# Cross attention beside a projection: earlier fetches, exponentials ahead of the last split, the next projection's operands split inside its last step

## The reference, cut to what matters

```python
s = einsum('bhsd,bhmd->bhsm', heads(xq), heads(mk)) * 128 ** -0.5
p = softmax(s, axis=-1)
xo = einsum('bhsm,bhmd->bhsd', p, heads(mv))
xo = merge_heads(rms_norm(xo, xattn_norm_w))
mixed = concatenate([gla_o, hgrn_o, xo], axis=-1)
mixed = mixed * silu(gate)
x = x + einsum('bse,ed->bsd', mixed, w_out)
```

## Time and profile before

| | us |
|---|---|
| median of 3 runs (2594.1 to 2599.44) | 2598.51 |
| the profiled execution's own time | 2591.98 |
| its span | 2590.2 |
| PE busy | 2432.3 (94%) |
| DVE, ACT, POOL busy | 1178.3, 910.4, 757.6 |
| idle time of PE before L1450, L1440 and L403 at this place | 14.6, 8.7, 6.8 |

### The profile page before, as it was taken

How to read it: one execution, slowest core, us unless ns; L and a number is a source line. 1 busy time by engine, 2 the same in 40 slices (tenths; PEclk the granted TensorE clock), 3 DMA queues, 4 the chain that set the end, 5 groups by cost and what they waited for, 6 DMA issues and landing times.

```text
span 2590.2 us, 42170 instructions
## 1 busy us (share of the span) xinstructions
PE 2432.3 (94%) x16392; PEld 2131.3 (82%) x16392; DVE 1178.3 (45%) x2536; ACT 910.4 (35%) x1685; POOL 757.6 (29%) x725
## 2 busy tenths in 40 slices
PE   6999989999997898899999999999999999798986
PEld 5778968798786898899998898777898777586786
DVE  3001359999994332400000155346435434666535
ACT  4214554444443332311212233433334333444321
POOL 3112325455641121312223133243223322221123
PEclk9999999999998999999999999999999999899998
DMA  4334334333335123232222313313321323636511
GB/s 181 123 110 153 114 134 147 129 127 124 114 131 211 58 81 114 82 113 93 92 95 97 126 50 122 110 62 109 119 92 71 127 92 125 219 138 221 205 50 65
DMA packets 153707, 306.01 MB, mean 118 GB/s; under 512 B 11456, under 2 KB 75584, under 8 KB 142288
## 3 DMA queue, kind: packets, MB, share of 16 engines
q1 hardware_dynamic: 89296, 215.77, 23.8%
q10 hardware_dynamic: 64256, 88.10, 9.5%
HBM read 204.22 MB, written 99.61 MB: 117 GB/s over the span
## 4 chain that ended last, share of the span: by engine, by line
PE 66%; issue 17%; DVE 9%; DMA 3%; POOL 3%; ACT 2%; ACTq 0%; SPq 0%; POOLq 0%; DVEq 0%
PE bank L392 10%; PE bank L394 9%; PE bank L393 9%; PE bank L403 7%; PE bank L404 7%; PE bank L405 7%; PE bank L1974 3%; PE bank L1954 2%; POOL w_lo L358 2%; PE bank L1374 1%; PE bank L1943 1%; PE bank L666 1%; DVE w_lo L358 1%; DVE rec_z L1109 1%; DMA rec_pre<-mixT 1%
## 5 line engine op out<-in xcount | busy, mean ns | idle before, releaser
L403 PE MATMUL bank<-w_hi,at_hi 128*128 128x256 f32 x2432 | 703.9, 289 | 15.0 <-DVE at_lo L2154 7.0
L404 PE MATMUL bank<-w_lo,at_hi 128*128 128x256 f32 x2432 | 691.2, 284 | 0.0
L405 PE MATMUL bank<-w_hi,at_lo 128*128 128x256 f32 x2432 | 691.1, 284 | 0.0
L392 PE MATMUL bank<-at_hi,w_hi 128*128 128x512 f32 x1472 | 609.4, 414 | 22.5 <-DVE at_lo L1574 8.5
L394 PE MATMUL bank<-at_hi,w_lo 128*128 128x512 f32 x1472 | 579.5, 394 | 0.0
L393 PE MATMUL bank<-at_lo,w_hi 128*128 128x512 f32 x1472 | 578.2, 393 | 0.0
L358 POOL TENSOR_TENSOR w_lo<-w_raw,w_hi 128x2048 fp32r<-128x2048 f32 x69 | 318.1, 4610 | 863.7 <-ACT w_hi L371 863.7
L403 PEld LDWEIGHTS bank<-w_hi,at_hi 128*128 128x128 f32 x2432 | 470.6, 194 | 29.2 <-issue 19.9
L404 PEld LDWEIGHTS bank<-w_lo,at_hi 128*128 128x128 f32 x2432 | 470.1, 193 | 0.6
L405 PEld LDWEIGHTS bank<-w_hi,at_lo 128*128 128x128 f32 x2432 | 469.6, 193 | 0.0
L423 ACT ACTIVATE stage<-bank 128x512 f32<-128x512 f32 x272 | 162.4, 597 | 640.7 <-PE bank L394 337.1
(11 more groups left out here) (251 smaller groups left out, 2969.2 us busy)
## 6 DMA issues: line engine op xcount, KB each, us to landing
w_raw<-in_weights SPq DMA_DIRECT2D x84, 1024.0 KB, 6.6
feat<-stage ACTq DMA_DIRECT2D x152, 256.0 KB, 2.0
tok<-stage ACTq DMA_DIRECT2D x104, 256.0 KB, 2.2
stage<-feat SPq DMA_DIRECT2D x32, 256.0 KB, 3.2
x<-in_x SPq DMA_DIRECT2D x4, 1024.0 KB, 9.7
w_mem<-in_w_mem SPq DMA_DIRECT2D x4, 1024.0 KB, 11.6
logg<-gate_g ACTq DMA_DIRECT2D x8, 512.0 KB, 2.8
rec_b<-logg SPq DMA_DIRECT2D x16, 256.0 KB, 4.7
```

Of the source, the lines that this page charges most:

```text
L392: nc.tensor.matmul(ps_gemm[i % 2], wh, ah, start=(k == 0), stop=False)
L403: nc.tensor.matmul(o, ah, wh, start=(k == 0), stop=False)
L404: nc.tensor.matmul(o, ah, wl, start=False, stop=False)
L405: last = nc.tensor.matmul(o, al, wh, start=False, stop=(k == KT - 1))
```

## The change

It touches five places:

- In the recurrence's last head SP issues load 3, keys, values and loads 4 to 6, each behind a wait of its own (`gate_silu`, `r_o`, `fill_lo`), ahead of the last store to `mixT`. ACT and DVE split load 3 together with loads 0 to 2.
- After the barrier SP issues the first head's queries, then the first half of X, then waits for the last store and issues the first head's gates, load 7, queries and gates of the second head, and the weights. ACT and DVE split loads 4 to 6 ahead of the first step; load 7 and the recurrence's last weight split move behind the first step's exponentials.
- The projection's parts per step are 2, 3, 1, 2 in the first and 1, 3, 1, 3 in the others.
- The next projection's first token half is split inside the last step (`rest_high`, `rest_low`), three row groups ahead of the sums of squares on ACT and ahead of the normed rows on DVE, five behind them. The rows of the last two heads are read from `ca_mx` itself and no longer go through DRAM. The second token half follows in phase 4.
- The loops of phase 3 are written out instead of turning on a register.

```diff
-        beside_cross = Beside(0, HEADS // 2, gemm_out[0], [1, 3, 1, 3] * 4)
+        beside_cross = Beside(0, HEADS // 2, gemm_out[0], [2, 3, 1, 2] + [1, 3, 1, 3] * 3)
...
                 fill_load(sp, mix_slots, mixT[0:D, :], FILLED0, range(3))
+                sp.wait_ge(gate_silu, 2 * (2 * HEADS))
+                fill_load(sp, mix_slots, mixT[0:D, :], FILLED0, range(3, 4))
+                sp.wait_ge(r_o, head * 8 + (6 + 8))
+                sp.dma_start(cmk[:].rearrange("p h m -> p (h m)"), mk_dram).then_inc(c_mem, 16)
+                sp.dma_start(cmv[:].rearrange("p t n -> p (t n)"), mv_dram).then_inc(c_mem, 16)
+                fill_load(sp, mix_slots, mixT[0:D, :], FILLED0, range(4, 7))
...
-                    fill_low(dve, mix_slots, FILLED0, range(3))
+                    fill_low(dve, mix_slots, FILLED0, range(4))
...
-                    fill_high(act, mix_slots, 0, range(3))
+                    fill_high(act, mix_slots, 0, range(4))
...
         def p3_sp(sp):
-            fill_load(sp, mix_slots, mixT[0:D, :], FILLED0, range(3, 4))
-            sp.dma_start(cmk[:].rearrange("p h m -> p (h m)"), mk_dram).then_inc(c_mem, 16)
+            block_stored(sp, REC_BLOCKS - 4)
+            queries_in(sp, 0, 0)
+            sp.dma_start(X[:, :, 0:HALF], I["x"].rearrange("(t p) d -> p t d", p=P)[:, :, 0:HALF]).then_inc(x_in, 16)
             sp.wait_ge(r_st, 16 * (2 * 2 * HEADS + 1))
             block_stored(sp, REC_BLOCKS - 2)
-            cross_load(sp, 0, 0)
-            sp.dma_start(cmv[:].rearrange("p t n -> p (t n)"), mv_dram).then_inc(c_mem, 16)
-            sp.dma_start(X[:, :, 0:HALF], I["x"].rearrange("(t p) d -> p t d", p=P)[:, :, 0:HALF]).then_inc(x_in, 16)
-            cross_load(sp, 0, 1)
+            gates_in(sp, 0, 0)
+            fill_load(sp, mix_slots, mixT[0:D, :], FILLED0, range(7, LOADS))
+            queries_in(sp, 0, 1)
+            gates_in(sp, 0, 1)
             beside_cross.weights(sp, 0)
-            fill_load(sp, mix_slots, mixT[0:D, :], FILLED0, range(4, LOADS))
...
+            sp.wait_ge(fill_lo, FILLED1)
+            fill_load(sp, rest_slots, mixT[D:2 * D, :], FILLED1, range(2))
+            for j in range(2):
+                sp.wait_ge(c_st[j], 16 * 2)
+            fill_load(sp, rest_slots, mixT[D:2 * D, :], FILLED1, range(2, 3))
             beside_cross.weights(sp, 1)
...
         def p3_act(act):
-            fill_high(act, mix_slots, 0, range(3, 4))
             all_products(act, gemm_rec)
-            split_high(act, *rec_block(REC_BLOCKS - 1))
-            fill_high(act, mix_slots, 0, range(4, LOADS))
-            with act.Fori(0, PAIRS) as it:
+            fill_high(act, mix_slots, 0, range(4, 7))
+            for it in range(PAIRS):
...
+                    if first:
+                        fill_high(act, mix_slots, 0, range(7, LOADS))
+                        split_high(act, *rec_block(REC_BLOCKS - 1))
                     beside_cross.results(act, it, 4 * n + 1)
...
+                    if final:
+                        rest_high(act, 0, range(3))
...
+                    if final:
+                        rest_high(act, 0, range(3, KT))
                     beside_cross.results(act, it, 4 * n + 3)
...
         def p3_dve(dve):
-            fill_low(dve, mix_slots, FILLED0, range(3, 4))
-            low_after(dve, REC_BLOCKS * 4 - 1)
-            fill_low(dve, mix_slots, FILLED0, range(4, LOADS))
-            with dve.Fori(0, PAIRS) as it:
+            fill_low(dve, mix_slots, FILLED0, range(4, 7))
+            for it in range(PAIRS):
...
+                    if first:
+                        fill_low(dve, mix_slots, FILLED0, range(7, LOADS))
+                        low_after(dve, REC_BLOCKS * 4 - 1)
                     beside_cross.sums(dve, it, 4 * n + 1)
...
+                    if final:
+                        rest_low(dve, 0, range(3))
                     dve.wait_ge(c_rs, it * 8 + (2 * n + 2))
...
+                    if final:
+                        rest_low(dve, 0, range(3, KT))
                     beside_cross.sums(dve, it, 4 * n + 3)
...
+        def rest_slice(k, h):
+
+            return cmx[:, k - 6, half(h)] if k >= 6 else rest_slots[k // 2][:, k % 2, :]
+
+        def rest_high(act, h, ks):
+
+            for k in ks:
+                if k == 0:
+                    act.wait_ge(tile_done, 4 * (gemm_out[0][0].first + gemm_out[0][0].n) + 6 + 2 * h)
+                if k < 6:
+                    act.wait_ge(part_in[k // 2], 16 * (h + 4))
+                else:
+                    act.wait_ge(c_mx, 4 * (PAIRS - 1) + (4 + 2 * (k - 6) + h + 1))
+                nc.scalar.activation(at_hi[:, k, half(h)], rest_slice(k, h), ACT.Copy).then_inc(fill_hi, 1)
...
         def p4_act(act):
-            all_products(act, gemm_out[0])
-            fill_high(act, rest_slots, 1, range(LOADS))
+            rest_high(act, 1, range(KT))
...
         def p4_dve(dve):
-            all_products(dve, gemm_out[0])
-            fill_low(dve, rest_slots, FILLED1, range(LOADS))
+            rest_low(dve, 1, range(KT))
```

More of the change, by code:

```diff
@@ L1424, in cross_load, with gates_in @@
             sp.dma_start(cq[:, j, :], feat1[XQ + head * P:XQ + (head + 1) * P, :]).then_inc(c_in[j], 16)
+        def gates_in(sp, it, j):
+            head = it * 2 + j
             sp.dma_start(cg[:, j, :], feat1[C_AT + head * P:C_AT + (head + 1) * P, :]).then_inc(c_in[j], 16)
         def p3_pe(pe):
-            with pe.Fori(0, PAIRS) as it:
+            ready = lambda k, h: FILLED0 + h * KT + k
+            for it in range(PAIRS):
                 for j, hf, n in halves():
-                    head = pe.snap(it * 2 + j)
-                    col = pe.snap(it * (2 * P) + j * P)
-                    beside_cross.products(pe, it, 4 * n, lambda k, h: FILLED0 + h * KT + k)
-                    if n == 0:
+                    head = it * 2 + j
+                    beside_cross.products(pe, it, 4 * n, ready)
+                    if it == 0 and n == 0:
                         pe.wait_ge(c_mem, 32)
@@ L1440, in p3_pe @@
                         last = nc.tensor.matmul(ps_a[:, b // 2, (b % 2) * MEM:(b % 2 + 1) * MEM], cq[:, j, t * P:(t + 1) * P],
-                                                cmk[:, bass.ds(head, 1), :].rearrange("p o m -> p (o m)"),
-                                                start=True, stop=True)
+                                                cmk[:, head, :], start=True, stop=True)
                     last.then_inc(c_s, 1)
-                    beside_cross.products(pe, it, 4 * n + 1, lambda k, h: FILLED0 + h * KT + k)
+                    beside_cross.products(pe, it, 4 * n + 1, ready)
                     pe.wait_ge(c_e, it * 16 + (4 * n + 8))
@@ L1457, in p3_pe @@
                             last = nc.tensor.matmul(ps_6[:, b * P:(b + 1) * P], cpT[:, b, m, :],
-                                                    cmv[:, m, bass.ds(col, P)], start=(m == 0), stop=(m == MT - 1))
+                                                    cmv[:, m, head * P:(head + 1) * P], start=(m == 0), stop=(m == MT - 1))
                     last.then_inc(c_o, 1)
-                    beside_cross.products(pe, it, 4 * n + 3, lambda k, h: FILLED0 + h * KT + k)
+                    beside_cross.products(pe, it, 4 * n + 3, ready)
                     pe.wait_ge(c_on, it * 4 + (n + 2))
@@ L1493, in p3_act @@
                                              scale=small[:, 16 + b:17 + b], accum_out=small[:, 20 + b:21 + b]).then_inc(c_ss, 1)
+                    if final:
+                        rest_high(act, 0, range(3, KT))
                     beside_cross.results(act, it, 4 * n + 3)
-                    if hf == 1:
+                    if hf == 1 and it < PAIRS - 1:
                         act.wait_ge(c_mx, it * 4 + (n + 5))
-                        act.dma_start(mixT[3 * 512:4 * 512, :][bass.ds(it * (2 * P) + j * P, P), :], cmx[:, j, :]).then_inc(c_st[j], 16)
-            for j in range(2):
-                act.wait_ge(c_st[j], 16 * (PAIRS + 1))
+                        head = it * 2 + j
+                        act.dma_start(mixT[3 * 512 + head * P:3 * 512 + (head + 1) * P, :], cmx[:, j, :]).then_inc(c_st[j], 16)
         def p3_pool(pool):
-            with pool.Fori(0, PAIRS) as it:
+            for it in range(PAIRS):
                 for j, hf, n in halves():
@@ L1510, in p3_dve @@
         def p3_dve(dve):
-            fill_low(dve, mix_slots, FILLED0, range(3, 4))
-            low_after(dve, REC_BLOCKS * 4 - 1)
-            fill_low(dve, mix_slots, FILLED0, range(4, LOADS))
-            with dve.Fori(0, PAIRS) as it:
+            fill_low(dve, mix_slots, FILLED0, range(4, 7))
+            for it in range(PAIRS):
                 for j, hf, n in halves():
+                    first, final = (it, n) == (0, 0), (it, n) == (PAIRS - 1, 3)
                     if n == 0:
@@ L1546, in p3_dve, with rest_low @@
                                                    ALU.mult).then_inc(c_mx, 1)
+        def rest_slice(k, h):
```

(11 more changed lines are left out.)

13 lines of the change are left out of this document (8 added, 5 removed).

## The result

| | before | changed |
|---|---|---|
| median, first comparison (4 runs each) | 2596.31 us | 2567.18 us |
| range of these runs | 2591.23 to 2599.44 | 2565.94 to 2568.24 |
| ratio, 95% interval | | 0.9888 [0.9871, 0.9904] |
| the profiled execution's own time, span | 2591.98, 2590.2 | 2568.24, 2566.4 |
| run again (5 runs; before 9 runs) | 2591.93 | 2569.40, ratio 0.9922 [0.9908, 0.9935] |

The changed kernel is faster by 22 to 29 us, depending on the runs of before it is set against; the profiled executions differ by 23.7. I use the profiled executions to say where the time came from, and ratios for how much it is.

A forecast was written before the change was run, and what follows sets the result against it. PE's stops around the cross attention, mainly for exponentials behind late loads and for the next projection, were taken as the bound; 13.4 + 8.1 = 21.5 us off 2598.51 gives 2577.0, range 2567 to 2586.

The forecast's parts named there:

- What bounds it: Around the cross attention PE stops 8.7 us ahead of scores, 14.6 ahead of transposes, 6.8 ahead of the next projection.
- Recurrence's end plus 1.2: At the recurrence's end, two more splits on ACT and DVE make the last store and barrier 1.2 us later.
- First scores 827.8, released by the gates behind X: First step's scores start at 827.8, 3.1 us later than before, waiting for gates that land after the 2 MB of X.
- rival in which the gates do not stand behind X: At the first scores: gates land early, scores at 823.3, gain 4.5 us more, 26.0 in all, 2572.5; chance 0.09.
- First step 18.0 us, the chain over ACT and DVE last: First step's L1464 comes 18.0 us after the scores, at 845.8, behind the chain after the exponentials; gain 13.4 us.
- rival in which the transfers eat this gain: First step: traffic beside the recurrence's stores or a longer chain leaves 5 to 8 us gain, about 2584; chance 0.13.
- Steps 2 to 7 nothing: Cross attention's later steps keep their parts, operations and length, so no gain or loss there.
- 366 further rows in PE's stream: Writing out the loops adds 366 rows to PE's stream; taking the branch away costs nothing visible.
- End 8.1: Last step to next projection: 9.0 us were lost before, 0.9 stays lost at the first tile; gain 8.1, bounds 9.0 and 4.6.
- rival in which POOL gets in first: Last step: POOL takes the port before DVE's last low piece, PE waits 4.4 us; gain 18.0, 2580.5; chance 0.16.
- The sum: Whole kernel: 13.4 + 8.1 = 21.5 us gain, taking the profiled execution from 2591.98 to 2570.5.
- The number given, 2577.0: Predicted time of the whole kernel: the 21.5 us gain taken from the shown runs' median of 2598.51.

The follow-up runs named there:

- The start alone: Changed kernel with the old end of the cross attention (no split of the next operand inside the last step, all four heads through DRAM): ratio to before 0.9942.
- the end alone: Changed kernel with the old start of the cross attention (transfers, splits and parts per step as before): ratio to before 0.9965.
- own semaphore: Changed kernel with the gates counting on another semaphore, so the scores wait for queries, keys and values only: ratio to before 0.9899.
- all three edits: Changed kernel with gates' separate semaphore, DVE's X wait behind the maxima, last weight split ahead of exponentials: ratio to before 0.9898; with 2, 2, 1, 3 parts 0.9891.

## Why the prediction was right, point by point

- **What bounds it.** Right. The two stops were ACT behind late loads and the operand of the next projection, and both went; the third, ahead of the scores, stayed, as forecast (10.0 instead of 8.7).
- **Recurrence's end plus 1.2.** Measured 1.2, over the path that was named: POOL's small operation again ended just behind DVE's last split.
- **First scores 827.8, released by the gates behind X.** Measured 827.42, gates landed at 827.35. From the recurrence's end it was 13.3 by my numbers and is 13.7. Putting the gates ahead of X moved the scores by 4.1 us (my price was 4.5): the mechanism is shown. The rival in which the gates do not stand behind X falls with it.
- **First step 18.0 us, the chain over ACT and DVE last.** Measured 17.32, the chain last with 1.3 us of stop (I had 1.5). Gain 13.4 by the prediction, 13.6 in the trace once the 0.85 us by which this execution was early is taken off. The start alone, on the same footing, gave 12.0 (13.2 less the 1.2 of the recurrence's end); of the difference 1.2 is its longer A, the rest its longer C. The 18.0 was not all rows: the priced links add up to 17.2, and 0.8 stood for POOL's addition and hops without a price of their own. The sums of squares began 13.4 us behind the scores instead of 13.8, and from there it took 3.9 instead of 4.2. The rival in which the transfers eat this gain falls: between 804 and 808 us they moved 409 GB/s and TensorE was busy all the time. What the prediction did not part is the new order and the earlier transfers: by the estimate above the transfers would have done without the order.
- **Steps 2 to 7 nothing.** The seven steps between took 117.48 and 117.41, and written-out loops gain nothing and cost nothing that the runs can tell. For the prediction's 366 further rows in PE's stream no row is shown.
- **End 8.1.** Measured 8.15 in the profile (101.48 and 93.33), the same for the end alone; against the other profiles with the old end it is 8.7 to 9.2, so that 8.15 hits 8.1 so closely is luck in part. Its pieces: POOL's low piece stood until DVE's fifth split was over and ended at 969.3, 7.2 us behind the last cross transposes as forecast, and the stop for the first tile's sum was 0.49 us, where I had 0.9. The rule of the Trainium skill (SBUF — State Buffer, Who interferes with whom), that the one of the two who issues first holds the port for the whole instruction, is borne out: POOL's 4.98 instead of 4.51, and two DVE splits in 4.46 instead of 1.3. The rival in which POOL gets in first did not happen in any of the nine profiles with the new end (C is 93.32 to 93.35 in all).
- **The sum.** 2570.5 for the profiled execution's own time; measured 2568.24. Of the 2.3 between, 0.85 lie ahead of the place, 0.7 in the first step, minus 0.5 in the wait for the gates, 0.1 in steps and end, and 1.1 behind it. That the terms' own errors are so small together is partly that 0.7 and 0.5 have opposite signs.
- **The number given, 2577.0, was 9.8 us too high**, and 2567.18 lies inside the range by 0.2 us only: that it does is luck. Most of the 9.8, 6.5 us, came from the base and not from a term: I took the gain from a median of three runs (2598.51), 6.5 us above the execution whose rows the terms came from, and more than thirty later runs of before put its median at 2591.5 to 2592. From 2592 the same terms give 2570.5. Of the other 3.3 us, 2.3 are those of the sum above, and 1.1 is that the median lies below the profiled execution. As a gain, 21.5 was forecast, and 22.5 was measured with both kernels run in turn.

## What to carry to other kernels

When a wait for one thing is removed, look in the same semaphore and in the same queue for what is late next: here the scores still waited for gates they do not use, because gates and queries counted on one semaphore and 2 MB stood between them in the queue; two further waits stood behind that one, each hidden until the one before it went. Moving an instruction ahead on a busy engine gives only part of the stop as long as the data that the instructions behind it want come late; and once those data come early, see whether the new order is still worth anything. Here no run has the early transfers with the old order, so that this stays an estimate. And where an execution's profile and the median of a few runs differ by more than the effect of a term, the terms' sum belongs to the profile's own base.

## What the runs showed of the hardware that was not expected

TensorE's granted clock at the recurrence's end was not the same in all profiles, though the instructions up to there were. The window 814.5 to 818.5 us in the kernel with the own semaphore, and then in the changed kernel (busy times, then clock):

```profile
814.50:818.50 4.00, 4.00 (x22) 4.00 (x23) 2.70 (x6) 3.28 (x6) 0.00 (x0) 0.60 0.97 320
```

```profile
814.50:818.50 4.00, 2.90 (x24) 2.70 (x23) 2.78 (x5) 3.23 (x6) 0.00 (x0) 1.00 1.00 354
```

The instructions up to there are the same, and so are TensorE's stops (1.8 and 0.3 us). In the first, 24 matmuls took 4.60 us, part of them at 1.2 GHz; in the second they took 3.1 us at 2.4 GHz. Of the eight profiles in which these 24 matmuls stand there, six have part of them at 1.2 GHz (4.3 to 4.6 us for the 24) and two, both of the changed kernel, have them at full clock (3.1 us). What decides it none of these runs shows, nor whether it goes by the kernel or by the execution. It moved no total here: in all eight TensorE stops behind them for the scores, 1.1 us at the least, so that the slower matmuls only shorten that stop.

The clock of the scores themselves goes with that stop. In the three kernels in which it lasted 1.1 to 1.8 us (own semaphore, and all three edits with either shares) the scores took 1.96 to 1.97 us, at 2.4 GHz; in the five in which it lasted 4.4 to 10.2 us they took 3.5 to 3.75.
